# Last expert stage ("memory"): two activation loads on the ScalarE queue, wide sums of squares, and the last choice handover rearranged

## What is computed

```python
# first block, attention of one query block
p = softmax(logits + bias, axis=-1)
o = p @ v
# between the blocks
x = rms_norm(x + gate_f * moe, g_final)          # end of the first block
h = rmsnorm(x, g_pre_mix) * (1 + sh_scale) + shift   # start of the second
# second block, peer: 8 heads, 128 x 128 keys, 16 experts a head
best, pos = top_k(top_k(s1)[:, :, None] + top_k(s2)[:, None, :])
gate = softmax(best)
y = sum over the 128 chosen experts e of  gelu(x . u[e]) * gate[e] * v[e]
```

## Time and profile before

| | us |
|---|---|
| median of three runs | 2821.68 |
| profiled execution | 2831.22 |
| its span, first to last instruction | 2829.4 |
| outside the span | 1.8 |

### The profile page before, as it was taken

One profiled execution on the slowest core, in us unless ns is written; L12 is line 12 of the kernel. 1 busy time (PEld: TensorE's weight loads), 2 busy tenths in 40 slices (PEclk: granted clock), 3 DMA queues, 4 the chain that ended last, 5 costly groups with the idle time before them and its releaser, 6 DMA issues. The chain is left out here.

```text
span 2829.4 us, 36912 instructions
## 1 busy us (share of the span) xinstructions
PE 2655.4 (94%) x14029; PEld 2170.7 (77%) x14033; DVE 1792.7 (63%) x3168; ACT 1075.5 (38%) x1724; POOL 927.0 (33%) x470
## 2 busy tenths in 40 slices
PE   6997998889989999999897999999999989999999
PEld 4775774333477878778785899999999978888887
DVE  6969432111141637429754099997888967888888
ACT  3325734222233332138633233334555533333333
POOL 0011122222214330112141357886322233445442
PEclk9997999999989999999998999999999999999999
DMA  8830048999633345300322136886699799999995
GB/s 320 330 119 1 1 154 310 417 372 384 260 116 119 134 172 194 120 30 1 120 90 91 60 139 247 304 287 225 209 311 323 292 389 368 374 385 386 385 382 217
DMA packets 135467, 646.27 MB, mean 228 GB/s; under 512 B 21536, under 2 KB 22432, under 8 KB 91040
## 3 DMA queue, kind: packets, MB, share of 16 engines
q1 hardware_dynamic: 86368, 483.80, 45.5%
q0 software_dynamic: 48384, 158.38, 14.9%
q10 hardware_dynamic: 576, 2.27, 0.2%
HBM read 620.25 MB, written 75.50 MB: 246 GB/s over the span
## 5 line engine op out<-in xcount | busy, mean ns | idle before, releaser
L195 PE MATMUL psum<-h_hi,w_hi 128*128 128x384 f32 (+1 forms) x1808 | 667.4, 369 | 33.2 <-DVE h_lo L570 8.7
L197 PE MATMUL psum<-h_hi,w_lo 128*128 128x384 f32 (+1 forms) x1808 | 654.5, 362 | 0.0
L196 PE MATMUL psum<-h_lo,w_hi 128*128 128x384 f32 (+1 forms) x1808 | 653.9, 362 | 0.0
L176 POOL TENSOR_TENSOR w_lo<-ring,w_hi 128x2048 fp32r<-128x2048 f32 x46 | 215.5, 4685 | 741.7 <-ACT w_hi L169 701.5
L195 PEld LDWEIGHTS psum<-h_hi,w_hi 128*128 128x128 f32 x1808 | 343.8, 190 | 70.0 <-issue 30.6
L196 PEld LDWEIGHTS psum<-h_lo,w_hi 128*128 128x128 f32 x1808 | 343.8, 190 | 33.0 <-issue 1.9
L197 PEld LDWEIGHTS psum<-h_hi,w_lo 128*128 128x128 f32 x1808 | 342.8, 190 | 33.9
L2572 ACT ACTIVATE w_hi<-ring 128x2048 fp32r<-128x2048 f32 x127 | 242.6, 1910 | 214.7 <-PE psum L197 197.4
L195 PE MATMUL psum<-w_hi,a_hi 128*128 128x512 f32 x768 | 300.8, 392 | 12.4 <-DVE w_lo L2580 11.8
L196 PE MATMUL psum<-w_lo,a_hi 128*128 128x512 f32 x768 | 299.7, 390 | 0.0
L197 PE MATMUL psum<-w_hi,a_lo 128*128 128x512 f32 x768 | 299.6, 390 | 0.0
(11 more groups left out here) (492 smaller groups left out, 4598.4 us busy)
## 6 DMA issues: line engine op xcount, KB each, us to landing
ring<-in_weights SPq DMA_DIRECT2D x199, 1024.0 KB, 7.9
w_expert_in<-in_experts_in SPq DMA_DIRECT2D x32, 2048.0 KB
hid_dram<-hid_acts SPq DMA_DIRECT2D x64, 384.0 KB
gates_dram<-block_gates SPq DMA_DIRECT2D x24, 1024.0 KB, 14.0
hid_tiles<-hid_dram SPq DMA_DIRECT2D x64, 384.0 KB
gate_tiles<-gates_dram SPq DMA_DIRECT2D x15, 1536.0 KB, 11.9
o<-in_ada_later SPq DMA_DIRECT2D x16, 1024.0 KB, 6.4
w_expert_down<-in_experts_down SPq DMA_DIRECT2D x16, 1024.0 KB
```

What stands on the lines that cost most here:

```text
L176: eng.tensor_tensor(lo, slot(k, n), hi.bitcast(F32), ALU.subtract).then_inc(k.w_ready, 1)
L195: k.nc.tensor.matmul(out, hi, x_hi, start=start, stop=False)
L196: k.nc.tensor.matmul(out, hi, x_lo, start=False, stop=False)
L197: return k.nc.tensor.matmul(out, lo, x_hi, start=False, stop=stop)
```

## The change

1. Attention: ScalarE's `scale_rows` of unit t-4 stands ahead of the exponentials of unit t in step t.
2. Between the blocks: the moving operand of the sums of squares is 128 columns wide in place of two. It lies in the memory of the diagonal, is set to ones as a whole, and its second column to the squared gain; the two sums are read from columns 0 and 1 of each block of 128.
3. Choice stage: the low half of tile 41 and the refill behind it leave the stage. VectorE makes the low half in the tail stage after its first `hot_rows`, and SyncE refills at the head of its tail stream. VectorE's wait for GpSimd's low half at the head of the tail is gone. The fourth tile's exponential stands after batch 37 in place of 38.
4. Output half: the loads of batches 2 and 3 go from SyncE's stream to ScalarE's, with the wait for `a_ready` there, and a wait for the stores. That of batch 2 stands after `high(1)`, that of batch 3 at the head of step 1.

```diff
@@ attention_stage, ScalarE
                     if 2 <= t < n + 2:
                         copy_turned(t - 2)
+                    if DEEP < t < first_sparse + DEEP + 1:
+                        scale_rows(t - DEEP - 1)
                     if t < n:
                         exp(t)
                         p, i = units[t]
                         if i == 1 and p < len(pairs) - 1:
                             split(index_pairs + p + 1)
-                    if DEEP < t < first_sparse + DEEP + 1:
-                        scale_rows(t - DEEP - 1)
@@ combine_projection_stage
-        weights, gain = sb("mid_weights", [P, KC, 2]), sb("mid_gain", [P, KC])
+        weights, gain = diagonal[:].rearrange("p a t n -> p (a t) n"), sb("mid_gain", [P, KC])
-        total = k.psum[:, sum_banks[0]:sum_banks[1] + 1, 0:4].rearrange("p j (i s) -> p j i s", s=2)
+        total = k.psum[:, sum_banks[0]:sum_banks[1] + 1, 0:PAIR].rearrange("p j (i n) -> p j i n", n=P)[:, :, :, 0:2]
-                            mm = nc.tensor.matmul(k.psum[:, sum_banks[j], 2 * i:2 * i + 2], square[:, c % 4, j * P:(j + 1) * P], weights[:, c],
+                            mm = nc.tensor.matmul(k.psum[:, sum_banks[j], i * P:(i + 1) * P], square[:, c % 4, j * P:(j + 1) * P], weights[:, c],
-                step(nc.vector.memset(weights[:, :, 0], 1.0))
+                step(nc.vector.memset(weights, 1.0))
@@ hidden_sync
-def hidden_sync(k, sp, b, r):
+def hidden_sync(k, sp, b, r, with_refill=True):
...
-    refill(k, sp, b + 2, r + 2)
+    if with_refill:
+        refill(k, sp, b + 2, r + 2)
@@ peer_choice_stage, SyncE, GpSimd, ScalarE
-                with sp.Fori(0, CHOICE_LOOPS[TT]) as g:
+                with sp.Fori(0, CHOICE_LOOPS[TT] - 1) as g:
                     for r in range(SLOTS):
                         hidden_sync(k, sp, SLOTS * g + r, r)
+                for b in range(early_batches - SLOTS, early_batches):
+                    hidden_sync(k, sp, b, b, b + 1 < early_batches)
...
-                    split_low(k, pool, b + 2)
+                    if b + 1 < early_batches:
+                        split_low(k, pool, b + 2)
...
-                    if b % SLOTS == SLOTS - 2:
+                    if b % SLOTS == 1:
                         exp(TT - 1)
@@ peer_tail_stage, SyncE
+            refill(k, sp, body * g0 + 1, body * g0 + 1)
             for i in range(body * rounds):
...
-            for b in range(2, 4):
-                sp.wait_ge(a_ready, b - 1)
-                load_hidden(b, b)
@@ peer_tail_stage, VectorE
-            wait_parts(k, dve, body * g0 + 1)
             dve.sem_inc(used, 2)
...
                         hot_rows(2 * steps * g + at)
+                        if not started and i == 0:
+                            split_low(k, nc.vector, body * g0 + 1)
@@ peer_tail_stage, ScalarE
+            def load_first(b):
+                act.wait_ge(k.hid_stored[b % 2], 16 + 16 * (b // 2 + 1))
+                act.wait_ge(a_ready, b - 1)
+                act.dma_start(hid[:, b % 2], k.hid_dram[b]).then_inc(hid_loaded[b % 2], 16)
+
             def step(b, r):
+                if r == 1:
+                    load_first(3)
                 if r + 1 < BATCHES:
                     act.wait_ge(batch_summed, b + 1)
                     high(b + 1, r + 1)
+                if r == 0:
+                    load_first(2)
```

## The result

The changed kernel takes **2819.2 us** (median of 20 runs, 2810.2 to 2823.5), the kernel before 2821.75 beside it. The ratio is **0.9979**, interval 0.9971 to 0.9988: 5.9 us faster, a fifth of a per cent (the two medians are only 2.6 us apart, the two means 4.6). A few runs that were over 1.5% above the fastest of their kernel are left out of all comparisons. I had forecast 2806.0 and a range that ended at 2818. The profiled execution took 2820.14 us, its span 2818.4, 11.0 less than the profiled span of before.

What follows compares the result with a forecast made beforehand. TensorE, busy 94% of the span, was taken as the bound. Gains of 1 (attention), 6 (sums), 5.7 (handover) and 3 (output half) made 15.7 us off the median 2821.68: 2806.0, range 2798 to 2818.

Steps and rivals of the forecast that it cites:

- rival (a): Sums of squares: the clock falls all the same, from gaps between turnings; gain 0, total 2812; chance 0.18.
- larger step: Handover: the choice stage ends earlier, with ScalarE last at 1979.7; 4.2 us, bounds 3.5 and 4.7.
- 1.5 for the clock: Handover: shorter idle time keeps most of the clock up afterwards; 1.5 us, bounds 0 and 2.2.
- Rival (c): Handover: VectorE pays for its 2.3 us and the clock falls anyway; gain 1.9, total 2809.8; chance 0.10.
- what is late next: Output half: batch 4, its activations and gates no earlier, can start at 2324.4 against 2326.8 before; difference 2.4 us.
- The lower bound of 0: Output half: gain 0 where stores are held up by the early loads sharing the engines; 3 us was taken.
- Rival (b): Output half: loads land no sooner, 16 busy engines being the limit; gain 0.5, total 2808.5; chance 0.12.
- Rival (d): Attention: exponentials behind the scaling make the next scores late; +38 us overall, total 2860; chance 0.05.
- its own rule: Whole kernel: bounds taken together, half of each lower bound's loss; 4 to 23 us of gain.

Runs made afterwards that it cites:

- width_2: The kernel before with only the sums and handover changes, but sums products 2 columns wide again; sums took 26.96 us.
- width_16: The kernel before with only the sums and handover changes, but sums products 16 columns wide; sums took 27.48 us.
- no_loads: The changed kernel with the loads of batches 2 and 3 back on SyncE's queue; ratio 0.9983 to the kernel before.

## Why the prediction was wrong

**Part 2** was right in the profile: forecast 6, and the sums take 6.6 us less in each profile but one (5.6), with the clock at 1.00 to the end of the spreading (it falls in the idle time behind it). The first products behind stayed at the lower clock at first, as said, and rival (a) is out. Of the rule of the Trainium skill (TensorE: Matmul & The Clock Gate, section The HAM clock gate: the clock follows how busy the array is) width_2 and width_16 say more than my trace did: by busy time they are as busy as the wide version, 7.80 of 7.80 and 8.30 of 8.30 us, and at half the clock. Read by busy time the rule fails here. The timed runs give this part less, 2.3 us, than its profiles do (see the sum).

**Part 3** was right in its larger step. I forecast 4.2 for the end of the stage and 1.5 for the clock; the idle time went from 6.66, on average of the four kernels without the part, to 3.14: 3.5 less, just at the lower of the bounds of 3.5 and 4.7. ScalarE, which I had through at 1979.7, became the slow one by some tenths, with a store of SyncE beside it. The clock is the term that was mis-sized. Right after the handover it stays up in 9 of 16 profiles with this part, and *choice rest* is 206.0; in the other seven it falls within 2 us of the restart, and once more 110 to 112 us behind it, and *choice rest* is 208.8 to 209.9. That is longer than the 207.7 to 208.1 without the part, where the clock falls once, in the idle time itself. On average that is 0.6, not 1.5. Rival (c) is out: VectorE did not pay. I had misplaced its slack: the 5.0 us stand before its third one-hot rows and not before the second, but they covered the low half all the same.

**Part 4** is the step whose mechanism failed. Its first half was right: load in 8.8 us (forecast 8.4), batch 2 earlier by 4.7 beyond the shift (forecast 5.4). The mistake is in "what is late next". I named batch 4 and its gates, and let the gates' load be no later than before. But the loads go ahead of the gates' stores on the same engines, the stores land 2.7 us later, and the gates' load and GpSimd's row 108 wait for them. I had counted row 108 nowhere: before, VectorE stood for batch 2's load until 2301.79 and came to row 108 only at 2309.41, when the row was there. With batch 2 early it comes sooner, and the row later: its gather goes out later, and takes 11.1 us to land in the changed kernel, 6.7 in no_loads. So the wait of batch 3 (in three of the seven profiles with both loads also one at batch 6) took back what batch 2 had won. The runs give 0.3 us of gain with 2 to both sides where I said 3; the profiles with both loads have tails of 636.1 to 640.5, 638.7 on average, and those without 637.1. The lower bound of 0, "where the stores are held up by the loads that now share the engines", was the right mechanism, and I gave it too little weight. Rival (b) is wrong too in its words: the loads did land sooner, and that its 0.5 us is near the 0.3 measured is luck.

The rule of the Trainium skill, DMA: Bandwidth & Descriptors, section Issuing engines are not separate DMA queues, that all issuing engines end on the same 16 DMA engines was the better guide to the sum, and the round between queues of its section Queues, rings and completion order to the single load. The trace agrees with both: 383 GB/s in the stretch where it was 402, so no more was moved, and 8.8 us for the load.

**Part 1** has the wrong sign: forecast 1 of gain, with bounds of 2 of loss and 3 of gain, measured 3.5 of loss, beyond the bounds (the 2 lies just within its interval). It is the largest piece of what is missing. The waits that I named did move. TensorE waits less for the scaling (8.9 for 12.4 us), ScalarE more for the reciprocal (21.4 for 15.6), which I had said would stay. The term that I put at nothing is the clock: it is low for 47.1 us of the attention on average of the four profiles with this part and for 41.7 in the sixteen without, and the stage is as long with it as without (135.0 and 135.3). That could account for a gain that does not come; that the reorder is what lowers the clock is argued from these averages and not tested. Where the loss of 3.5 lies is not shown, and its cause stays open. *Middle*, which the part does not touch, is 415.9 with it and 413.4 without, but with a standard deviation of 2.4 to 2.8 from profile to profile that makes this no proof. Rival (d) had the sign and was far off in size.

**The sum.** 15.7 was forecast, 5.9 to 7.3 measured: part 1 is 4.5 worse, part 4 2.7, and parts 2 and 3 gave 9.3 for 11.7. How the 9.3 divide stays open: the timed runs put 2.3 on part 2 and 7.0 on part 3, each within about 2, the profiles 6.6 and 4.1. The two differ by more than that interval, and only the sums are near one another (9.3 and 10.7). So the forecast's terms for parts 2 and 3 are borne out by the profiles, and by the timed runs only in their sum.

The range did not follow its own rule either. The lower bounds lose 3, 6, 2.2 and 3 us, 14.2 together; half of that leaves 8.6 us of gain, not 4, so that the rule would have ended the range at 2813.

## What to carry to other kernels

When a transfer is made earlier on full DMA engines, list what is pushed behind it and who waits for that, before you count the gain: here a store was pushed, and two waits hung on it. Time won at one wait is won only as far as the next transfer allows, so free the next one in the same edit (row 108 here, with one early load), and look at the stretch's end, not at the wait. A float32 product with a 128 x 128 stationary operand and a result of two columns was as dear here as one of 128 columns (0.118 and 0.116 us at full clock), and cost the clock; look at the granted clock, and try it wide. And do not credit a reorder with the waits that it shortens: here TensorE's wait for the scaling fell from 12.4 to 8.9 us, and the stage was as long as before.

## What was unexpected of the hardware

- **Width and clock.** With 2 and with 16 columns the clock was at 0.50 in a stretch in which TensorE was busy throughout; with 128 columns it was at 1.00.
- **The clock after a short stand.** After 3.14 us of idle time, the same code took 206.0 us in nine profiles and 208.8 to 209.9 in seven, with nothing between. In an idle time of 6.6 to 6.7 us the clock fell each time, and the code took 207.7 to 208.1.
- **Chance.** The 550 us ahead of the sums, the same instructions but for part 1, took 544.7 to 554.9 us from one profile to the next, about the spread of the timed runs (sd 3 to 6 us). An effect of 3 us there can't be read from two profiles.
